# Two stacked transformer blocks in one kernel: the last tile ahead of each of six post-norms by halves of the tokens, and a later wait for two places of the normed activations

## The reference

```python
for i in range(DEPTH):                                     # DEPTH = 2
    a = rms_norm(h, pre_mix_norm[i])
    m = hgrn2_mixer(a, ...) if i == 0 else mla_mixer(a, ...)
    h = h + rms_norm(m, post_mix_norm[i])                  # "mix"
    f = squared_relu_mlp(rms_norm(h, pre_mlp_norm[i]), w_mlp_in[i], w_mlp_out[i])
    h = h + rms_norm(f, post_mlp_norm[i])                  # "mlp"
    e = p[i] @ w_ple_proj[i]
    g = jax.nn.sigmoid(h @ w_ple_gate[i])
    h = h + rms_norm(g * e, ple_norm[i])                   # "ple"
```

## Time and profile before

| | |
|---|---|
| median of three runs | 2308.73 us |
| the profiled execution, whole | 2309.96 us |
| its span | 2308.2 us |
| mean granted clock of TensorE | 0.997 |
| VectorE, ScalarE, GpSimd busy | 56%, 28%, 68% |

### The profile page before, as it was taken

The page is one execution under the profiler, slowest core; times in us unless marked ns, Lnnn a source line. Parts: engine busy times, 40 slices in busy tenths (PEclk is TensorE's granted clock), DMA queues, the critical chain, the costliest instruction groups (busy, mean ns, idle before and its releaser), DMA issues.

```text
span 2308.2 us, 27603 instructions
## 1 busy us (share of the span) xinstructions
PE 2274.4 (99%) x10430; PEld 1852.0 (80%) x10430; DVE 1284.8 (56%) x1823; ACT 653.0 (28%) x1204; POOL 1575.7 (68%) x1532
## 2 busy tenths in 40 slices
PE   8999999999998999999999999999999999999998
PEld 6888878888886788888788888788668788888887
DVE  7774746335345777176545264469875445626354
ACT  3443432101013455154311011142344232202113
POOL 8666568777776455545597777678327937878784
PEclk9999999999999999999999999999999999999999
DMA  5222222333322111211233233323112312323332
GB/s 171 79 74 86 69 92 92 105 96 98 98 98 83 55 38 44 77 34 60 73 125 101 99 110 101 96 88 110 60 37 87 124 60 90 98 96 96 98 96 76
DMA packets 112725, 200.16 MB, mean 87 GB/s; under 512 B 12496, under 2 KB 21200, under 8 KB 112592
## 3 DMA queue, kind: packets, MB, share of 16 engines
q1 hardware_dynamic: 109424, 194.72, 26.5%
q10 hardware_dynamic: 3168, 3.67, 0.5%
HBM read 196.24 MB, written 2.10 MB: 86 GB/s over the span
## 4 chain that ended last, share of the span: by engine, by line
PE 93%; DVE 3%; POOL 2%; ACT 1%; DMA 0%; issue 0%; SPq 0%; DVEq 0%; POOLq 0%
PE bank L479 27%; PE bank L481 27%; PE bank L480 27%; POOL wL L2783 1%; PE bank L917 1%; PE bank L1041 1%; DVE bank L1937 1%; DVE h L1929 1%; PE bank L577 1%; PE bank L512 1%; PE bank L581 1%; POOL wH L2781 1%; PE bank L582 1%; DVE aL L1937 1%; PE bank L886 1%; PE bank L887 1%
## 5 line engine op out<-in xcount | busy, mean ns | idle before, releaser
L2783 POOL TENSOR_TENSOR wL<-raw,wH 128x512 fp32r<-128x512 f32 (+2 forms) x732 | 1009.5, 1379 | 61.1
L2781 POOL TENSOR_SCALAR wH<-raw 128x512 fp32r<-128x512 f32 (+2 forms) x732 | 530.3, 724 | 557.1 <-PE bank L481 478.5
L479 PE MATMUL bank<-aH,wH 128*128 128x512 f32 x1376 | 546.2, 397 | 8.9 <-DVE aL L1937 7.5
L481 PE MATMUL bank<-aH,wL 128*128 128x512 f32 x1376 | 536.8, 390 | 0.0
L480 PE MATMUL bank<-aL,wH 128*128 128x512 f32 x1376 | 536.6, 390 | 0.0
L479 PE MATMUL bank<-uH,wH 128*128 128x512 f32 (+1 forms) x978 | 378.5, 387 | 0.0
L481 PE MATMUL bank<-uH,wL 128*128 128x512 f32 (+1 forms) x978 | 376.8, 385 | 0.0
L480 PE MATMUL bank<-uL,wH 128*128 128x512 f32 (+1 forms) x978 | 376.7, 385 | 0.0
L479 PEld LDWEIGHTS bank<-aH,wH 128*128 128x128 f32 x1376 | 258.4, 188 | 68.4 <-POOL wL L2783 6.5
L480 PEld LDWEIGHTS bank<-aL,wH 128*128 128x128 f32 x1376 | 258.6, 188 | 56.7 <-issue 4.1
L481 PEld LDWEIGHTS bank<-aH,wL 128*128 128x128 f32 x1376 | 258.4, 188 | 54.9
(11 more groups left out here) (327 smaller groups left out, 3201.8 us busy)
## 6 DMA issues: line engine op xcount, KB each, us to landing
raw<-in_ws SPq DMA_DIRECT2D x698, 256.0 KB, 2.5
raw<-in_ws SPq DMA_DIRECT2D x24, 192.0 KB, 2.3
h<-in_xT SPq DMA_DIRECT2D x8, 256.0 KB, 5.9
E<-in_memT ACTq DMA_DIRECT2D x16, 128.0 KB, 2.5
raw<-in_ws SPq DMA_DIRECT2D x10, 128.0 KB, 2.1
tmp<-in_pT ACTq DMA_DIRECT2D x4, 256.0 KB, 3.1
out<-c_F SPq DMA_DIRECT2D x2, 512.0 KB, 2.9
out<-c_F SPq DMA_DIRECT2D x2, 384.0 KB, 2.9
```

Source lines behind the costliest of these rows:

```text
L479: P.e.matmul(o, lH, rH, start=start, stop=False, skip_group_check=skip)
L481: return P.e.matmul(o, lL, rH, start=False, stop=stop, skip_group_check=skip)
L2781: G.e.tensor_scalar(H, x, 1.0, 0.0, MUL, ADD).then_inc(*G.did("wH", n))
L2783: G.e.tensor_tensor(L, x, H.bitcast(F32), SUB).then_inc(*G.did("w", n))
```

## The change

A helper `linear_halves` on TensorE computes one output tile in two passes: tokens 0 to 255 and then 256 to 511, each 24 matmuls of 256 columns, in a PSUM bank of its own. It replaces `linear` for the eighth tile ahead of each of the six post-norms. ScalarE and VectorE take these halves as they come: copy or add, square (`square_half`). In the "ple" norm VectorE makes the square of the second half, which was ScalarE's, and ScalarE's preload of the table of Ln and Exp follows the second sigmoid directly. `stat_end` sums the last square by halves, each with its own wait. The weight piece of the tile's first four input tiles is given back in the second pass. In `add_normed` of the "mix" and "mlp" norms ScalarE waits for `p used` ahead of tile 6 and not of tile 0, VectorE at step 7 and not at step 1.

```diff
+            def linear_halves(event, freed, name, layer, c0, xH, xL, ready, ks=K8):
+
+                w = block(name, layer, ks, ((c0, 128),))
+                for half in range(2):
+                    c = half_cols(half)
+                    b = take(*event, half)
+                    for k, (H, L, n, end) in enumerate(w):
+                        P.wait_ge(G, "w", n)
+                        ready(k)
+                        i = three(b.ap[:, 0:256], H, L, xH[:, k, c], xL[:, k, c], k == 0, k == len(w) - 1)
+                        if half and end and k < len(w) - 1:
+                            i.then_inc(*P.did("w", n))
+                    i.then_inc(*P.did(*event, half))
+                    give(b, *freed, half)
+                P.also("w", w[-1][2])
...
-                if tail:
+                if adds:
+                    for half in range(2):
+                        c = half_cols(half)
+                        P.wait_ge(V if half and sid[0] == "ple" else A, "sq", sid, 7, half)
+                        i = P.e.matmul(b.ap[:, c], ones, sq[:, c], start=False, stop=half == 1, skip_group_check=True)
+                elif tail:
...
-                for o in range(3, 8):
+                for o in range(3, 7):
                     linear(("gate", i, o), (A, "sg", i, o), "w_ple_gate", i, 128 * o, aH, aL, hs_ready)
+                linear_halves(("gate", i, 7), (A, "sg", i, 7), "w_ple_gate", i, 128 * 7, aH, aL, hs_ready)
...
+            def square_half(sid, half):
+
+                c = half_cols(half)
+                A.wait_ge(V, "sum", sid, 6)
+                do(sq[:, c], F[:, 7, c], ACT.Square).then_inc(*A.did("sq", sid, 7, half))
+                squares_end[1] = (P, "stat", *sid)
...
                 rstd(1024, *sid)
-                A.wait_ge(*free)
                 for k in range(8):
+                    if k == (6 if free[1] == "p used" else 0):
+                        A.wait_ge(*free)
                     A.wait_ge(V, "h", src, k)
...
+                A.wait_ge(V, "Fg", i, 5)
+                for half in range(2):
+                    A.wait_ge(P, "gate", i, 7, half)
+                    do(mr[1][:, half_cols(half)], bk("gate", i, 7, half)[:, 0:256], ACT.Sigmoid).then_inc(*A.did("sg", i, 7, half))
+                    if half == 0:
+                        A.wait_ge(V, "Fg", i, 7, 0)
+                        square_half(("ple", i), 0)
                 exp_table()
...
                 for k in range(9):
-                    if k == 1:
+                    if k == (7 if free[1] == "p used" else 1):
                         V.wait_ge(*free)
...
+            def into_half(half, *event):
+                c = half_cols(half)
+                V.wait_ge(P, *event, half)
+                tt(F[:, 7, c], F[:, 7, c], bk(*event, half)[:, 0:256], ADD).then_inc(*V.did("F", *event, half))
...
+                for half in range(2):
+                    c = half_cols(half)
+                    V.wait_ge(A, "sg", i, 7, half)
+                    tt(F[:, 7, c], E[:, 7, c], mr[1][:, c], MUL).then_inc(*V.did("Fg", i, 7, half))
+
+                V.wait_ge(V, "Fg", i, 7, 1)
+                V.wait_ge(V, "sum", ("ple", i), 6)
+                tt(sq[:, c], F[:, 7, c], F[:, 7, c], MUL).then_inc(*V.did("sq", ("ple", i), 7, 1))
```

More of the change, by code:

```diff
@@ L511, in stat_end @@
                 P.wait_ge(cs_in)
-                i = P.e.matmul(b.ap[:, 0:n], ones, sums[:, 0:n], start=True, stop=not tail)
-                if tail:
+                i = P.e.matmul(b.ap[:, 0:n], ones, sums[:, 0:n], start=True, stop=not tail, skip_group_check=bool(adds))
+                if adds:
[4 more added lines that the diff above has]
+                elif tail:
                     P.wait_ge(A, "sq", sid, tiles - 1)
@@ L784, in mlp_ple @@
                     downs("w_mlp_out", i, tuple(range(8 * g, 8 * g + 8)), g == 0, lambda o: ("down", i, g, o),
-                          lambda o: (V if g else A, "F", "down", i, g, o), u_ready)
+                          lambda o: (V if g else A, "F", "down", i, g, o), u_ready, tiles=7 if g == 3 else 8)
+                    if g == 3:
+                        linear_halves(("down", i, g, 7), (V, "F", "down", i, g, 7), "w_mlp_out", i, 128 * 7, uH, uL, u_ready,
+                                      ks=tuple(range(8 * g, 8 * g + 8)))
                     P.also("down done", i, g)
@@ L806, in mlp_ple @@
                 return lin
-            for o in range(3, 8):
+            for o in range(3, 7):
                 linear(("ho", o), (A, "F", "ho", o), "hg_w_out", 0, 128 * o, uH, uL, y1_ready)
+            linear_halves(("ho", 7), (A, "F", "ho", 7), "hg_w_out", 0, 128 * 7, uH, uL, y1_ready)
             P.also("ho done")
@@ L933, in o_ready @@
                     P.wait_ge(V, "moL", 8 * half + k)
-                for o in range(8):
+                for o in range(7 if half else 8):
                     linear(("mw", half, o), (V if half else A, "F", "mw", half, o), "mla_w_o", 0, 128 * o, uH, uL, o_ready,
                            ks=tuple(range(8 * half, 8 * half + 8)))
+                if half:
+                    linear_halves(("mw", 1, 7), (V, "F", "mw", 1, 7), "mla_w_o", 0, 128 * 7, uH, uL, o_ready, ks=tuple(range(8, 16)))
                 P.also("mla out", half)
@@ L1517, in mlp_ple @@
                             p_split(i, 1)
-                        if g == 3:
+                        if g == 3 and o < 7:
                             A.wait_ge(V, "F", "down", i, g, o)
                             square(("mlp", i), o, F[:, o, :])
+                for half in range(2):
+                    A.wait_ge(V, "F", "down", i, 3, 7, half)
+                    square_half(("mlp", i), half)
                 embedded(4)
@@ L1523, in mlp_ple @@
                 embedded(5, 6, 7)
-                for o in range(8):
+                for o in range(7):
                     A.wait_ge(P, "gate", i, o)
@@ L1543, in act @@
                 square(("mix", 0), o, F[:, o, :])
+            for half in range(2):
+                A.wait_ge(P, "ho", 7, half)
+                do(F[:, 7, half_cols(half)], bk("ho", 7, half)[:, 0:256], ACT.Copy).then_inc(*A.did("F", "ho", 7, half))
+                A.wait_ge(A, "F", "ho", 7, half)
+                square_half(("mix", 0), half)
             mlp_ple(0, lambda k: vv("pre_mix_norm", 8 + k))
@@ L1669, in act @@
                 square(("mix", 1), o, F[:, o, :])
+            for half in range(2):
+                A.wait_ge(V, "F", "mw", 1, 7, half)
+                square_half(("mix", 1), half)
             A.also("end mla")
@@ L2240, in mlp_ple @@
                     for o in range(8):
-                        into(g == 0, o, "down", i, g, o)
+                        if g < 3 or o < 7:
+                            into(g == 0, o, "down", i, g, o)
                         if i == 1 and g == 0 and 0 < o < 7:
@@ L2254, in mlp_ple @@
                             add_squares(("mlp", i), o)
+                for half in range(2):
+                    into_half(half, "down", i, 3, 7)
                 add_normed(f"hs{i}", ("mlp", i), (P, "p used", i, 1), lambda k: vv("post_mlp_norm", 8 * i + k), None)
-                for o in range(8):
+                for o in range(7):
                     V.wait_ge(A, "sg", i, o)
@@ L2428, in dve @@
                     add_squares(("mix", 1), o)
+            for half in range(2):
+                V.wait_ge(A, "F", "mw", 0, 7)
+                into_half(half, "mw", 1, 7)
             V.also("end mla")
```

## The result

| | kernel before | kernel changed |
|---|---|---|
| median (13 runs each, one chip) | 2308.32 us | 2303.82 us |
| ratio, 95% interval | | 0.9979 (0.9971 to 0.9986) |
| the profiled execution, whole / span | 2309.96 / 2308.2 us | 2303.01 / 2300.9 us |
| mean granted clock | 0.997 | 0.998 |

The change takes 4.5 us off the median, 0.2%, and both ends of the interval lie under 1: 3.2 to 6.7 us. The forecast was 2303.3, 5.4 less than 2308.73. A second measurement beside other kernels gave 0.9977 (0.9968 to 0.9986), 5.2 us. The spans of the two profiled executions differ by 7.3 us, more than the medians. So first the question is where the 7.3 are, and then which of them belong to the change.

The account below looks back on a forecast made before the run. TensorE, busy 99%, bounds the kernel; its waits stand around the post-norms, mostly behind VectorE. Terms -1.01 x 3 - 1.42 - 1.03 + 0 = -5.5, rounded to -5.4, take 2308.73 to 2303.3 us; range 2301.0 to 2305.6.

Parts of the forecast that it names:

- The tile by halves, +0.32 each: Last tile ahead of each post-norm: 48 matmuls of 256 columns instead of 24 of 512 cost 0.32 us more.
- VectorE's idle time of 1.33 and 1.26 goes whole: Between VectorE's first and second normed tile: 1.33 us goes at "mix" layer 0 and both "mlp", 1.26 at "mix" layer 1.
- "mix" of layer 1, halves -0.16: Ahead of that norm's sum: tile cost 0.32 against 0.48 saved by half add and square, -0.16 us.
- "ple" of layer 1, 0: At that norm GpSimd is the bound, so halves' cost and shorter wait lie under it: 0 us.
- "ple" of layer 0, -1.03 with product and square at 0.46 each: From last tile to Ln: half product and square on VectorE bring Ln 1.03 us sooner, between -1.1 and -0.2.
- rival 2: "ple" norm of layer 0: Ln waits for ScalarE to drain around the table load, gain 1.03 goes, 2304.4; chance 0.12.
- The gain stays as long as the clock does the same: Product behind "ple" norm of layer 0: TensorE runs behind VectorE, so the 1.03 us lasts if the clock is unchanged.
- Rival 1: Clock stays up at "ple" norm of layer 0: TensorE ends by the last low part, 1.8 us more, 2301.5; chance 0.17.

Follow-up runs that it names:

- run with 16 matmuls: Changed kernel plus 16 matmuls of 512 columns that nobody reads, in TensorE's gap at the "ple" norm of layer 0: 2302.82 us, ratio 0.9974.

## Why the prediction was right, and where it was wrong

The time was forecast as 2303.3 and came out at 2303.82. Part of that closeness is luck: the forecast took 5.4 us off 2308.73, the measured gain was 4.5 off 2308.32. Point by point:

- **The tile by halves, +0.32 each.** Right: 0.31 to 0.38 in stretches B, C and G.
- **VectorE's idle time of 1.33 and 1.26 goes whole.** Right, and the bound was named rightly: ScalarE's wait alone gives nothing. The size was low: 5.25 us gross forecast, 5.69 measured. With the later wait alone the last low part ends 1.38 us sooner behind P at "mix" of layer 0, 1.48 at "mlp" of layer 0 and 1.39 at "mix" of layer 1, as the stretches lose 1.37, 1.49 and 1.37. The idle time that went gives 1.30, 1.30 and 1.22 of that; the rest is that the meeting with GpSimd cost less. At "mix" of layer 0 the first low part fell from 1.27 to 1.19 us; at "mlp" it fell from 1.28 to 0.68 and the second rose from 0.69 to 1.10; at "mix" of layer 1 the first fell from 1.27 to 1.12.
- **"mix" of layer 1, halves -0.16.** Right: -0.17 in E.
- **"ple" of layer 1, 0.** Right, and for the reason given: H is 81.82 with halves, 81.81 without. P of ple 1 comes 0.32 later and the stretch from there to N is 0.32 shorter. N follows the start of GpSimd's work behind the "mlp" norm by 61.70 to 61.79 us in the ten profiles with VectorE's square or whole tiles. With the square on ScalarE (four profiles) it follows by 61.50 to 61.57, since VectorE's square, 1.37 us there too, had also held up GpSimd: its operation right behind took 0.79 us in the changed kernel and 0.61 with the square on ScalarE.
- **"ple" of layer 0, -1.03 with product and square at 0.46 each.** Wrong. This is the step that failed, at "I take 0.46 each, with 0.42 and 0.85 as ends": the product took 0.57 us and the square 1.37, far outside the ends. From the start of the product to the end of the square 1.97 us went by (740.73 to 742.70) where 0.96 was reckoned, and that is the 1.0 that the sum is off here. Ln came 0.27 earlier behind P, P itself 0.31 later, together +0.04 and not -1.03. I had taken the half operations' price from rows with an input in PSUM, and GpSimd was at work here. My rival 2 had this as a side case, "if VectorE's two half operations take 0.85 each"; the table load was never the chain in the changed kernel.
- **"The gain stays as long as the clock does the same".** The path is right: the prediction has TensorE end behind VectorE's low parts at this norm, and in ten of the 14 profiles TensorE's own time, with half of the low clock in it, decides. VectorE's low parts do so in the three where the clock stayed up and in one with a short low time and a product that began 1.1 us sooner. The condition did not hold: the low clock under TensorE's work took 5.98 us before and 3.41 after, and it varies like this without an edit. Rival 1 (the clock stays up) came halfway: it fell, but for 3.4 and not 6.8 us in both profiles. Its price was near: 1.8 us were reckoned for a clock that stays up, and D of the kernel before was 1.64 above VectorE's time. What the run with 16 matmuls says of the prediction in its rival is not exact: the prediction took VectorE's low parts as the bound only for a clock that stays up.

The errors cancel in part. Measured by stretches and without the clock: -5.69 for the waits, +0.33 at three tiles, -0.17, and 0.01 for the gate of layer 0, where the product starts 0.30 sooner behind a P that is 0.31 later. That is -4.9, beside medians of -4.5 and -5.2. The forecast -5.4 had 0.44 too little for the waits and 1.0 too much for the gate.

The 7.3 us between the two profiles consist of about 4.7 of this kind, 1.3 from the shorter low clock (half of 5.98 us before, of 3.41 after), and 1.25 from the program's start, since P of mix 0 stood 0.92 sooner in spite of a tile that costs 0.33. One profile against one other would have credited the change with 2.5 us that it doesn't earn.

## What to carry to other kernels

Follow a wait of the busiest engine to the engine that is late next, and move that one's wait: here ScalarE's wait was the visible one and gave 0 alone, VectorE's gave 4.8 alone, both 5.8 us. Splitting a tile costs a fixed amount for each further matmul (0.31 to 0.38 us for 24), and pays only where the engine behind it waits for the last piece. Price a short VectorE operation from rows with the same places of its inputs and with GpSimd doing the same beside it, and read a gain of 1 us from stretches between fixed events of several profiles, not from the ends of two.

## What the runs showed of the hardware that was not expected

- A VectorE operation of 256 columns on two SBUF inputs that started inside a GpSimd operation ended 0.27 us behind the end of that, so it took up to 1.37 us and not 0.42 to 0.43; with one input in PSUM it took 0.42 inside one.
- With a gap of TensorE of 3.8 to 4.3 us went a low clock of either 3.4 us (three profiles) or 6.8 us (eight), which began between 4.3 and 7.3 us behind P of ple 0, in the gap or just behind it. Between two profiles with the same gate's norm (halves alone, and the changed kernel again) this was worth 1.3 us of D.
- No drain showed in front of or behind the table load: in the kernel with the square on ScalarE it starts 0.02 us after the square's end and Ln 0.01 after its own.
